# Constant loads, tile padding and start-up order in a three-layer fp32r kernel on one core

## The chip, the cores and the metric

The kernel runs on one core of a Trainium2 chip. The metric is the device time of one execution in microseconds (us). TensorE is called PE here, VectorE DVE, ScalarE ACT, GpSimd POOL, SyncE SP.

## The reference, cut to what matters

256 tokens of width 2048 go through three layers. Each layer is a norm, a large input projection, a mixer, and an output projection that is added to the residual; the last layer has also a gated feed-forward part.

```python
# first block: layer AB (banded and dilated attention), layer C (2-D neighbourhood attention)
x = x + (attention_ab(rmsnorm(x) @ w_in_ab) * silu(z)) @ w_out_ab
x = x + (attention_c(rmsnorm(x) @ w_in_c) * silu(z)) @ w_out_c
x = _rmsnorm(x, ln_f)
# second block
h = rmsnorm(x, norm1_w) @ w_in
x = x + concat(pool_mixer(h), gated_deltanet(h), rglru_mixer(h)) @ w_out
x = x + conv_ffn(rmsnorm(x, norm2_w), ffn_up, ffn_conv_w, ffn_down)
return rmsnorm(x, final_norm_w)
```

## The kernel before, in words

**Panels and chunks.** Every large product is cut into panels of 512 weight columns, 87 in all, numbered through the kernel: 0 to 12 `w_in_ab`, 13 to 16 `w_out_ab` (AT_OUT_AB is 13), 17 to 32 `w_in_c`, 33 to 36 `w_out_c` (AT_OUT_C is 33), 37 to 46 `w_in`, 47 to 50 `w_out`, and from 51 three groups of 12 for the feed-forward part. A panel has four chunks of 512 weight rows. I write (33,2) for chunk 2 of panel 33.

**Precision split.** Each fp32 weight chunk is split in two fp32r parts: ACT copies `raw` to `w_hi` (`split`, L335, the copy at L333), and DVE subtracts to get `w_lo` (L694 to L696). The activations are split the same way, into `act_hi`/`act_lo` or `ff_hi`/`ff_lo`. PE runs three of the four partial products, 48 matmuls for each chunk of an input projection (`panel`, L1308: the weight is stationary, 256 token columns move; L1321, L1323, L1329) and 24 for each chunk of an output projection (`deproject`, L1338: the activation is stationary, 512 weight columns move; L1356 to L1358). The panels 13 to 16 and 33 to 36 have `ff_hi`/`ff_lo` as the stationary operand, the other output panels `act_hi`/`act_lo`.

**Queues.** All order is written out by hand, with semaphores. SP loads the weights (`load`, L264): `raw` has one slot for each chunk of a panel, so the load of (g,c) waits for the DVE split of (g-1,c). ACT may write `w_hi` for (g,c) when PE has used chunk two before (`w_used`, L338), and DVE follows it. In an output panel PE starts a chunk only when both halves are there (L1350, L1351); in an input panel the `w_lo` matmuls come after those with `w_hi`.

**Start.** ACT issues three row tables (L636) and the sinks (L637), SP the identity (L291), `x` (L285) and the first weights (L289). PE waits for all five constants on one semaphore (L1659), transposes the tables, and ACT copies them to `params` (L639). Then each of the four chunks of panel 0 needs its quarter of `x` transposed by PE (`turn`, L1367), scaled into `act_hi` by ACT (`high_of_x`, L402) and into `act_lo` by DVE (`low_of_x`, L778). ACT also squares `x` (`squares_of`, L355) for the norm; DVE and ACT make the root (`variance`, `root`, `inverse_root`, `diagonal`), and PE spreads the scale over the partitions (`spread_scale`, L1395), after chunk 3 of panel 0.

**End of an attention layer.** `finish` (ACT L470, DVE L864) gates the heads with silu(z) and splits them into `ff_hi` and `ff_lo`, in four steps beside the last input panel and the first chunks of panel 13 or 33. Right behind it on ACT's queue stand loads: after the first layer `cmask` (L660) and the biases of two heads (`start_bias(1)`, eight small DMAs at L421), after the second `ln_f` (L670) and eight constants of the second block (`load_middle`, L488, issued at L500). Only then does `sum_into` (L388) go on with the weight split of (13,2) or (33,2).

**Tiles.** SBUF tiles are allocated one after the other (L113 to L134). In bytes for each partition all sizes are multiples of 64 but two: `params` (337 x 4 = 1348) and `gates` (172 x 4 = 688). Behind them lie `ones`, `scale_diag`, `token_scale`, `squared`, `proj`, `ff_gate`, `ff_hi` and `ff_lo`; ahead of them `resid`, `act_hi`, `act_lo`, `raw`, `w_hi`, `w_lo`, `work`, `ident`. The first tile starts at a multiple of 64 bytes, and the allocator rounds each start up to a multiple of 32. So all tiles behind `params` start 32 bytes past a multiple of 64, those ahead of it on one.

Of the kernel before, what the change touches and what calls it, by code (L numbers as in the profile page):

```python
# [24 lines left out]
P = 128  # L25
S = 256
D = 2048
NT = S // P
NK = D // P
PANEL = 512  # L30
QK = 4
HEADS = 16
A_HEADS = 8
# [68 lines left out]
def program(nc, a):  # L102

    ctx = ExitStack()
    with ctx:
        def sb(name, shape, dt=F32):
            return ctx.enter_context(nc.sbuf_tensor(name, shape, dt))
# [12 lines left out]
        ident = sb("ident", [P, P])  # L120
        params = sb("params", [P, PR_END])
        sinks = sb("sinks", [P, HEADS])
        small = sb("small", [P, 256])
        gates = sb("gates", [P, 172])
        ones = sb("ones", [P, P])
# [14 lines left out]
        x_landed = [sem(f"x_landed{i}") for i in range(4)]  # L140
        const_landed = sem("const_landed")
        raw_landed = [sem(f"raw_landed{c}") for c in range(4)]
# [4 lines left out]
        scale_diag_ready, scale_mm, scale_out = sem("scale_diag_ready"), sem("scale_mm"), sem("scale_out")  # L147
        turned, hi_act, lo_act = sem("turned"), sem("hi_act"), sem("lo_act")
        params_turned, params_ready = sem("params_turned"), sem("params_ready")
        z_ready = sem("z_ready")  # L150
# [112 lines left out]
        def _(sp):  # L263
# [19 lines left out]
            def load_x(i):  # L283
                cols = slice(i * PANEL, (i + 1) * PANEL)
                sp.dma_start(resid[:, :, cols], x_rows[:, :, cols]).then_inc(x_landed[i], 16)  # L285

            def load_first(c):
                src = a["w_in_ab"][c * 512:(c + 1) * 512, 0:PANEL].rearrange("(k p) n -> p k n", p=P)
                sp.dma_start(raw[:, c, :, :], src).then_inc(raw_landed[c], 16)  # L289

            sp.dma_start(ident[:], a["ident"]).then_inc(const_landed, 16)  # L291
            load_x(0)
            load_first(0)
            load_x(1)
            load_x(2)
            load_first(1)
            load_x(3)
            load_first(2)
            load_first(3)
            for p, (col, _) in enumerate(AB_PANELS):  # L300
                if p > 0:
                    load(False, p, rows_of(a["w_in_ab"]), slice(col, col + PANEL))
            panels(a["w_out_ab"], AT_OUT_AB, N_OUT)
            with sp.Fori(0, HEADS // 4) as j:
                for kind in range(3):
                    load(False, 3 * j + (AT_C + kind), rows_of(a["w_in_c"]), bass.ds(j * PANEL + kind * D, PANEL))
            panels(a["w_in_c"], AT_C + 12, 4, col0=3 * D)
            panels(a["w_out_c"], AT_OUT_C, N_OUT)
            for p, panel in enumerate(IN2_PANELS):
# [21 lines left out]
        def _(act):  # L331
# [55 lines left out]

            def sum_into(k, gp0, gain=None, x_hi=None, last=False):  # L388


                for i in range(N_OUT):
                    def between(c):
                        if c == 1 and i > 0:
                            summed_squares(k, gp0, i - 1)
                        if c == 2 and i > 0 and x_hi is not None:
                            high_of_x(k, i - 1, gain, x_hi)
                    panel(gp0 + i, between, last=last and i == N_OUT - 1)
                summed_squares(k, gp0, N_OUT - 1)
                if x_hi is not None:
                    high_of_x(k, N_OUT - 1, gain, x_hi)  # L400
# [22 lines left out]

            def start_bias(layer):
                if layer == 1:
                    act.wait_ge(rpb_spread, 16)
                for b in range(2):
                    load_bias(layer, b, b)

# [40 lines left out]
            def finish(layer, gp):  # L470
# [15 lines left out]
                high(layer, 3)  # L486

            def load_middle():  # L488

                for out, src in (  # L490
                        (work[:, 20:26, :], a["mid_consts"]),
                        (consts[:, M_POOLW:M_POOLW + POOL_G, :], a["pool_w_2"].rearrange("g c d -> c g d")),
                        (lru_w[:, 0:LRU_B, :], a["lru_wa_2"].rearrange("g c d -> c g d")),
                        (lru_w[:, LRU_B:2 * LRU_B, :], a["lru_wx_2"].rearrange("g c d -> c g d")),
                        (counts, a["counts"]),
                        (gate_w.rearrange("p (k n) -> p k n", k=NK),
                         a["w_in_2"][:, IN2_GATES:IN2_GATES + 12].rearrange("(k p) n -> p k n", p=P)),
                        (a_log, row_of(a["gdn_a_log_2"], GDN_H)),
                        (dt_bias, row_of(a["gdn_dt_bias_2"], GDN_H))):
                    act.dma_start(out, src).then_inc(mid_landed, 16)  # L500

# [132 lines left out]
            for i in range(3):  # L634
                rows = a[f"rows{i}"]
                act.dma_start(work[0:rows.shape[0], i, 0:P], rows).then_inc(const_landed, 16)  # L636
            act.dma_start(sinks[:, 0:A_HEADS], row_of(a["sink_a"], A_HEADS)).then_inc(const_landed, 16)  # L637
            act.wait_ge(params_turned, 3)
            copy(params[:, 0:PR_END], aux[:, 0, 0:PR_END]).then_inc(params_ready, 1)  # L639
            for c in range(4):  # L640
                high_of_x(0, c, PR_LN_AB, act_hi)
                split(0, c, first=c < 2)
                squares_of(0, c)
            root(0)
            for c in range(2):
                split(1, c)

            act.dma_start(rpb_rows, bass.AP(tensor=a["rpb_c"].tensor, offset=0,
                                            ap=[[RPB, HEADS], [0, GRID_W], [1, RPB]])).then_inc(rpb_spread, 16)
            start_bias(0)  # L650
            def first_root(k):
# [7 lines left out]
            finish(0, AT_AB + N_AB - 1)  # L659
            act.dma_start(cmask, a["cmask"]).then_inc(mask_landed, 16)  # L660
            start_bias(1)
            sum_into(1, AT_OUT_AB, PR_LN_C, act_hi)
            for p in range(3):
# [4 lines left out]
            finish(1, AT_C + N_C - 1)  # L668
            act.wait_ge(gated, 8)
            act.dma_start(lnf, row_of(a["ln_f"], D)).then_inc(lnf_landed, 16)  # L670
            load_middle()
            sum_into(2, AT_OUT_C, PR_N1, act_hi)
# [15 lines left out]
        def _(dve):  # L688
# [482 lines left out]

            chain.link(nc.vector.memset(ones[:], 1.0))
            chain.link(nc.vector.memset(sinks[:, A_HEADS:HEADS], NEG))
            dve.wait_ge(const_landed, 16 * 5)
            dve.wait_ge(params_ready, 1)
            for c in range(4):
                low_of_x(0, c, PR_LN_AB, act_hi, act_lo)
                split(0, c)
            variance(0, 1e-5)
            inverse_root(0)  # L1180
            diagonal(0, rstd)
            split(1, 0)
            scale_row(0)
            dve.wait_ge(w_used, 4)
            to_tile(AB_PANELS[0][1], 0)
            split(1, 1)
            for p in range(1, N_AB - 1):
# [117 lines left out]
        def _(pe):  # L1305
# [89 lines left out]
            def spread_scale(k):  # L1395
                pe.wait_ge(scale_diag_ready, k + 1)
                mm(aux[:, 1, 0:S], ones[:], scale_diag[:].rearrange("p t n -> p (t n)"), start=True, stop=True
                   ).then_inc(scale_mm, 1)

            def first_of(k, gp0=0):  # L1400

                def amid(c):
# [3 lines left out]
                    elif k > 0 and c == 0:  # L1406
                        turn_summed(k, gp0, 3)
                    if c == 3:
                        spread_scale(k)
# [248 lines left out]

            pe.wait_ge(const_landed, 16 * 5)  # L1659
            at = 0  # L1660
# [110 lines left out]
```

## Time and profile before

| | us |
|---|---|
| median of 3 runs (lowest, highest) | 2268.82 (2266.54, 2269.53) |
| the profiled execution's own time | 2265.74 |
| its span in the trace | 2263.5 |
| PE, PE weight loads, busy | 2189.7, 2070.8 |
| DVE, ACT, POOL, busy | 1261.8, 888.2, 206.6 |
| mean granted clock of TensorE | 0.989 of full speed |

The profile is one execution. Busy times are sums over the span; PE's matmuls overlap, so the spacing of their starts and the gaps between them tell more than the busy share.

### The profile page before, as it was taken

To read this page: it belongs to the slowest core of one execution; us is meant where nothing else is said; L and a number is where in the kernel's file an instruction comes from. 1 tells how busy PE (TensorE), PEld (TensorE's weight loads), DVE (VectorE), ACT (ScalarE), POOL (GpSimd) and SP (SyncE) were. 2 spreads that over 40 slices of the span, in tenths; PEclk is the share of its full clock that TensorE was granted. 3 is DMA by queue.
4 is the path that set the end of the run, shared out by engine and by line. 5 is a ranking of instruction groups with operands and counts; after the bars stand their busy time and mean duration, and the time that the engine had idled before them with its cause. 6 is when DMAs were issued, how large, how long until landed. Compare 5 with 4: busy or idle time off the path is not lost.

```text
span 2263.5 us, 36570 instructions
## 1 busy us (share of the span) xinstructions
PE 2189.7 (97%) x15751; PEld 2070.8 (91%) x15751; DVE 1261.8 (56%) x1265; ACT 888.2 (39%) x850; POOL 206.6 (9%) x242
## 2 busy tenths in 40 slices
PE   6999999999999998999999889999999999999997
PEld 6999998899999997789999878999989999899986
DVE  4555555544555555565588645565445655466554
ACT  4344334443333344453546324434333333333333
POOL 0101100002022110002000420001100011000200
PEclk9999999999999999999999999999999999999999
DMA  6755544555555546554554105555555555555553
GB/s 221 220 176 171 168 163 163 186 173 182 167 168 168 181 156 201 173 181 149 168 168 150 56 9 188 194 186 187 186 188 185 185 187 186 191 182 186 186 187 111
DMA packets 212140, 386.66 MB, mean 171 GB/s; under 512 B 26058, under 2 KB 29595, under 8 KB 211739
## 3 DMA queue, kind: packets, MB, share of 16 engines
q1 hardware_dynamic: 185552, 369.19, 49.6%
q10 hardware_dynamic: 26443, 15.30, 2.4%
q8 instruction: 120, 1.97, 0.4%
q14 instruction: 25, 0.20, 0.0%
HBM read 382.36 MB, written 4.00 MB: 171 GB/s over the span
## 4 chain that ended last, share of the span: by engine, by line
PE 90%; DVE 4%; ACT 3%; ACTq 1%; issue 1%; POOL 0%; DMA 0%; DVEq 0%; POOLq 0%
PE acc L1321 20%; PE acc L1323 20%; PE acc L1329 20%; PE acc L1356 8%; PE acc L1357 8%; PE acc L1358 7%; ACT w_hi L333 2%; DVE w_lo L696 1%; PE aux L1448 1%; ACTq L421 1%; PE aux L1426 1%; PE aux L1610 1%; PE aux L1619 1%; PE aux L1373 1%; PE aux L1437 1%
## 5 line engine op out<-in xcount | busy, mean ns | idle before, releaser
L696 DVE TENSOR_TENSOR w_lo<-raw,w_hi 128x2048 fp32r<-128x2048 f32 x348 | 810.9, 2331 | 795.9 <-ACT w_hi L333 795.2
L333 ACT ACTIVATE w_hi<-raw 128x2048 fp32r<-128x2048 f32 x348 | 666.1, 1915 | 1079.2 <-PE acc L1329 752.5
L1321 PE MATMUL acc<-act_hi,w_hi 128*128 128x256 f32 x2496 | 618.4, 288 | 8.5 <-ACT w_hi L333 8.5
L1323 PE MATMUL acc<-act_lo,w_hi 128*128 128x256 f32 x2496 | 608.9, 284 | 0.0
L1321 PEld LDWEIGHTS acc<-act_hi,w_hi 128*128 128x128 f32 x2496 | 481.5, 193 | 10.7 <-DVE act_lo L783 9.4
L1323 PEld LDWEIGHTS acc<-act_lo,w_hi 128*128 128x128 f32 x2496 | 481.7, 193 | 1.2
L1321 PE MATMUL acc<-ff_hi,w_hi 128*128 128x256 f32 x1536 | 372.9, 283 | 0.6 <-issue 0.6
L1323 PE MATMUL acc<-ff_lo,w_hi 128*128 128x256 f32 x1536 | 372.6, 281 | 0.0
L1329 PE MATMUL acc<-act_hi,w_lo 128*128 128x256 f32 x2496 | 325.8, 283 | 0.0
L1329 PEld LDWEIGHTS acc<-act_hi,w_lo 128*128 128x128 f32 x2496 | 310.8, 192 | 0.2
L1323 PEld LDWEIGHTS acc<-ff_lo,w_hi 128*128 128x128 f32 x1536 | 289.6, 189 | 0.1
L1321 PEld LDWEIGHTS acc<-ff_hi,w_hi 128*128 128x128 f32 x1536 | 288.7, 188 | 1.1 <-issue 1.0
L1329 PE MATMUL acc<-ff_hi,w_lo 128*128 128x256 f32 x1536 | 199.9, 282 | 0.0
L1356 PE MATMUL acc<-w_hi,act_hi 128*128 128x512 f32 x512 | 199.9, 390 | 0.0
L1358 PE MATMUL acc<-w_hi,act_lo 128*128 128x512 f32 x512 | 199.3, 389 | 0.0
L1357 PE MATMUL acc<-w_lo,act_hi 128*128 128x512 f32 x512 | 199.2, 389 | 0.0
L1329 PEld LDWEIGHTS acc<-ff_hi,w_lo 128*128 128x128 f32 x1536 | 191.1, 188 | 0.1
L1231 POOL COPY work<-proj 128x256 f32<-128x256 f32 (+1 forms) x96 | 63.8, 704 | 669.8 <-DVE proj L718 569.0
L1356 PE MATMUL acc<-w_hi,ff_hi 128*128 128x512 f32 x256 | 103.9, 406 | 18.7 <-DVE w_lo L696 18.7
L1356 PEld LDWEIGHTS acc<-w_hi,act_hi 128*128 128x128 f32 x512 | 96.1, 188 | 20.1 <-issue 0.2
L1358 PEld LDWEIGHTS acc<-w_hi,act_lo 128*128 128x128 f32 x512 | 96.1, 188 | 20.0
L1357 PEld LDWEIGHTS acc<-w_lo,act_hi 128*128 128x128 f32 x512 | 96.1, 188 | 19.9 <-issue 0.2
(247 smaller groups left out, 1680.7 us busy)
## 6 DMA issues: line engine op xcount, KB each, us to landing
raw<-in_ffn_up SPq DMA_DIRECT2D x96, 1024.0 KB, 5.2
raw<-in_w_in_c SPq DMA_DIRECT2D x64, 1024.0 KB, 5.6
raw<-in_w_in_ab SPq DMA_DIRECT2D x52, 1024.0 KB, 5.1
raw<-in_ffn_down SPq DMA_DIRECT2D x48, 1024.0 KB, 5.1
raw<-in_w_in SPq DMA_DIRECT2D x40, 1024.0 KB, 5.1
raw<-in_w_out_ab SPq DMA_DIRECT2D x16, 1024.0 KB, 5.1
raw<-in_w_out_c SPq DMA_DIRECT2D x16, 1024.0 KB, 5.0
raw<-in_w_out SPq DMA_DIRECT2D x16, 1024.0 KB, 5.1
```

The lines of the kernel that those rows point to most:

```text
L333: copy = lambda out, in_, **k: nc.scalar.activation(out, in_, ACT.Copy, **k)
L421: act.dma_start(bias(b)[r * GRID_W:(r + 1) * GRID_W, t, :] .rearrange("p (a k) -> p a k", a=4), src).then_inc(rpb_landed[b], 16)
L696: tt(w_lo[:, c % 2], raw[:, c], w_hi[:, c % 2].bitcast(F32), ALU.subtract).then_inc(lo_ready, 1)
L1231: ins = copy(out, proj[:, tile, :])
L1321: mm(out(j), w, hi[:, 4 * c + k, :], start=(c == 0 and k == 0 and j % 2 == 0), stop=False, skip_group_check=True)
L1323: mm(out(j), w, lo[:, 4 * c + k, :], start=False, stop=False, skip_group_check=True)
L1329: ins = mm(out(j), w_lo[:, c % 2, k, j * P:(j + 1) * P], hi[:, 4 * c + k, :], start=False, stop=(c == 3 and k == QK - 1), skip_group_check ...
L1356: mm(out(t), x_hi, w_hi[:, c % 2, k, :], start=(c == 0 and k == 0), stop=False)
L1357: mm(out(t), x_hi, w_lo[:, c % 2, k, :], start=False, stop=False)
L1358: ins = mm(out(t), x_lo, w_hi[:, c % 2, k, :], start=False, stop=(c == 3 and k == QK - 1))
L1373: ins = nc.tensor.transpose(aux[:, 2 * (i % 2) + j // 2, (j % 2) * S + t * P:(j % 2) * S + (t + 1) * P], rows[:, t, (4 * i + j) * P:(4 * i ...
L1426: ins = mm(aux[:, b, t * S:(t + 1) * S], qs(b)[:, t * P:(t + 1) * P], ks(b), start=(t == 0), stop=True, skip_group_check=True)
```

## The change

Six edits. (1) `params` and `gates` are padded to 352 and 176 columns. (2) The sinks have a semaphore of their own, and the wait for constants is for four DMAs. (3) SP's first loads alternate `x` and weights. (4) ACT squares `x` in pairs, the splits of panel 1 come ahead of the root, and `spread_scale(0)` moves behind chunk 0 of panel 1. (5) `cmask` is issued by SP at panel 2; the biases of the first two heads are issued by ACT at the last chunk of panels 14 and 15; `ln_f` and the constants of the second block are issued by SP, behind the loads of panel 33 and a wait for the last gating. (6) PE runs 16 matmuls on `ones` ahead of its first wait for data.

```diff
-        params = sb("params", [P, PR_END])
+        params = sb("params", [P, -(-PR_END // 16) * 16])
-        gates = sb("gates", [P, 172])
+        gates = sb("gates", [P, 176])
...
@@ SP
+            def load_middle():
...
+                    sp.dma_start(out, src).then_inc(mid_landed, 16)
...
-            load_x(0)
-            load_first(0)
-            load_x(1)
-            load_x(2)
-            load_first(1)
-            load_x(3)
-            load_first(2)
-            load_first(3)
+            for c in range(4):
+                load_x(c)
+                load_first(c)
             for p, (col, _) in enumerate(AB_PANELS):
                 if p > 0:
                     load(False, p, rows_of(a["w_in_ab"]), slice(col, col + PANEL))
+                if p == 2:
+                    sp.dma_start(cmask, a["cmask"]).then_inc(mask_landed, 16)
...
-            panels(a["w_out_c"], AT_OUT_C, N_OUT)
+            load(False, AT_OUT_C, rows_of(a["w_out_c"]), slice(0, PANEL))
+            sp.wait_ge(gated, 8)
+            sp.dma_start(lnf, row_of(a["ln_f"], D)).then_inc(lnf_landed, 16)
+            load_middle()
+            for i in range(1, N_OUT):
+                load(False, AT_OUT_C + i, rows_of(a["w_out_c"]), slice(i * PANEL, (i + 1) * PANEL))
@@ ACT
+                        if also:
+                            also(i, c)
...
-            def start_bias(layer):
-                if layer == 1:
-                    act.wait_ge(rpb_spread, 16)
-                for b in range(2):
-                    load_bias(layer, b, b)
+            def first_biases(i, c):
+
+                if c == 3 and 1 <= i <= 2:
+                    load_bias(1, i - 1, i - 1)
...
-            act.dma_start(sinks[:, 0:A_HEADS], row_of(a["sink_a"], A_HEADS)).then_inc(const_landed, 16)
+            act.dma_start(sinks[:, 0:A_HEADS], row_of(a["sink_a"], A_HEADS)).then_inc(sinks_landed, 16)
...
                 split(0, c, first=c < 2)
-                squares_of(0, c)
+                if c % 2 == 1:
+                    squares_of(0, c - 1)
+                    squares_of(0, c)
+            split(1, 0)
             root(0)
-            for c in range(2):
-                split(1, c)
+            split(1, 1)
...
-            act.dma_start(cmask, a["cmask"]).then_inc(mask_landed, 16)
-            start_bias(1)
-            sum_into(1, AT_OUT_AB, PR_LN_C, act_hi)
+            act.wait_ge(rpb_spread, 16)
+            sum_into(1, AT_OUT_AB, PR_LN_C, act_hi, first_biases)
...
-            act.wait_ge(gated, 8)
-            act.dma_start(lnf, row_of(a["ln_f"], D)).then_inc(lnf_landed, 16)
-            load_middle()
             sum_into(2, AT_OUT_C, PR_N1, act_hi)
@@ DVE
             variance(0, 1e-5)
+            split(1, 0)
             inverse_root(0)
             diagonal(0, rstd)
-            split(1, 0)
+            split(1, 1)
             scale_row(0)
             dve.wait_ge(w_used, 4)
             to_tile(AB_PANELS[0][1], 0)
-            split(1, 1)
+            dve.wait_ge(sinks_landed, 16)
@@ PE
+            def warm_up():
+
+                pe.wait_ge(ones_ready, 1)
+                for i in range(16):
+                    mm(aux[:, 3, 0:P], ones[:], ones[:], start=True, stop=True)
...
-                    if c == 3:
+                    if k > 0 and c == 3:
                         spread_scale(k)
...
-                    for p in range(1, 4):
+                    panel(1, 1, *x, amid=lambda c: spread_scale(0) if c == 0 else None)
+                    for p in range(2, 4):
                         panel(p, p % 2, *x, heads(p))
...
-            pe.wait_ge(const_landed, 16 * 5)
+            warm_up()
+            pe.wait_ge(const_landed, 16 * 4)
```

## Rows read from the trace of the kernel before

**Rows 1.** The page: busy us (share of the span) xinstructions
```profile
PE 2189.7 (97%) x15751; PEld 2070.8 (91%) x15751; DVE 1261.8 (56%) x1265; ACT 888.2 (39%) x850; POOL 206.6 (9%) x242
```

**Rows 2.** PE's waits: line waited for, us in total, times, longest
```profile
PE acc L1356 <- DVE w_lo L696: 18.7, 2, 13.1
PE aux L1663 <- DMA sinks<-in_sink_a: 9.1, 1, 9.1
```

**Rows 3.** ACT, and one row of DVE: start us, us, line, operation, idle before
```profile
372.01 1.06 ACT L333 ACTIVATE ff_hi<-proj 128x1024 fp32r<-128x1024 f32 x1 [2.73 <-DVE proj L857]
372.39 5.35 ACTq L421 DMA_DIRECT2D work<-scratch_rpb_rows  x8
373.10 1.23 DVE L861 TENSOR_TENSOR ff_lo<-proj,ff_hi 128x1024 fp32r<-128x1024 f32 x1 [1.12 <-ACT ff_hi L333]
377.84 3.71 ACT L333 ACTIVATE w_hi<-raw 128x2048 fp32r<-128x2048 f32 x2 [4.78 <-issue]
...
890.03 1.06 ACT L333 ACTIVATE ff_hi<-proj 128x1024 fp32r<-128x1024 f32 x1 [2.73 <-DVE proj L857]
890.04 0.34 ACTq L670 DMA_DIRECT2D proj<-in_ln_f  x1
...
891.96 3.42 ACTq L500 DMA_DIRECT2D work<-in_lru_wx  x1
...
902.74 0.46 ACTq L500 DMA_DIRECT2D small<-in_gdn_dt_bias  x1
903.30 3.71 ACT L333 ACTIVATE w_hi<-raw 128x2048 fp32r<-128x2048 f32 x2 [12.20 <-issue]
```

**Rows 4.** Stretches: PE busy (x), PEld, DVE, ACT, POOL, granted clock, DMA share, GB/s
```profile
365.20:376.61 11.41, 11.41 (x50) 8.86 (x48) 7.41 (x6) 4.87 (x4) 0.00 (x0) 1.00 0.65 221
...
382.22:388.28 6.06, 6.06 (x14) 4.82 (x15) 2.06 (x1) 0.00 (x0) 0.00 (x0) 0.50 0.83 282
388.28:407.00 18.72, 18.72 (x81) 15.05 (x80) 8.10 (x4) 5.76 (x3) 0.00 (x0) 1.00 0.38 134
894.63:907.68 13.05, 0.00 (x1) 0.03 (x1) 2.44 (x2) 3.71 (x2) 0.00 (x0) 0.59 0.70 194
907.68:910.53 2.85, 2.85 (x7) 2.27 (x8) 2.05 (x1) 0.00 (x0) 0.00 (x0) 0.50 0.52 162
2166.00:2230.00 64.00, 64.00 (x284) 53.03 (x283) 32.96 (x17) 24.13 (x21) 4.95 (x2) 1.00 0.56 190
55.05:72.33 17.28, 17.28 (x146) 17.28 (x145) 6.88 (x3) 5.75 (x3) 0.00 (x0) 1.00 1.05 309
1459.13:1510.97 51.84, 51.84 (x435) 51.84 (x434) 34.13 (x41) 17.25 (x9) 0.00 (x0) 1.00 0.57 182
```

**Rows 5.** The page: split groups, xcount | busy, mean ns; output matmuls on ff_hi
```profile
L696 DVE TENSOR_TENSOR w_lo<-raw,w_hi 128x2048 fp32r<-128x2048 f32 x348 | 810.9, 2331 | 795.9 <-ACT w_hi L333 795.2
L333 ACT ACTIVATE w_hi<-raw 128x2048 fp32r<-128x2048 f32 x348 | 666.1, 1915 | 1079.2 <-PE acc L1329 752.5
L1356 PE MATMUL acc<-w_hi,ff_hi 128*128 128x512 f32 x256 | 103.9, 406 | 18.7 <-DVE w_lo L696 18.7
```

**Rows 6.** SP in time at panel 34; the page: w_out_c loads, us to landing
```profile
881.28 6.99 SPq L271 DMA_DIRECT2D raw<-in_w_out_c  x2
...
raw<-in_w_out_c SPq DMA_DIRECT2D x16, 1024.0 KB, 5.0
```

**Rows 7.** The chain at the start, in order: start us, us, what
```profile
2.22 6.81 DMA sinks<-in_sink_a
...
10.44 1.98 PE aux L1373 x8
12.45 1.57 ACT act_hi L333 x4
14.02 1.81 ACT w_hi L333
```

**Rows 8.** ACT in panel 0: start us, us, line, operation, idle before
```profile
22.56 1.57 ACT L333 ACTIVATE act_hi<-aux,params 128x256 fp32r<-128x256 f32 x4 [5.53 <-PE aux L1373]
...
44.15 1.28 ACT L380 ACT_TABLE_LOAD   x1
```

More of the change, by code:

```diff
@@ L140, in program @@
         x_landed = [sem(f"x_landed{i}") for i in range(4)]
-        const_landed = sem("const_landed")
+        const_landed, sinks_landed = sem("const_landed"), sem("sinks_landed")
         raw_landed = [sem(f"raw_landed{c}") for c in range(4)]
@@ L148, in program @@
         turned, hi_act, lo_act = sem("turned"), sem("hi_act"), sem("lo_act")
+        ones_ready = sem("ones_ready")
         params_turned, params_ready = sem("params_turned"), sem("params_ready")
@@ L285, in load_x @@
                 sp.dma_start(resid[:, :, cols], x_rows[:, :, cols]).then_inc(x_landed[i], 16)
+            def load_middle():
+                for out, src in (
+                        (work[:, 20:26, :], a["mid_consts"]),
+                        (consts[:, M_POOLW:M_POOLW + POOL_G, :], a["pool_w_2"].rearrange("g c d -> c g d")),
+                        (lru_w[:, 0:LRU_B, :], a["lru_wa_2"].rearrange("g c d -> c g d")),
+                        (lru_w[:, LRU_B:2 * LRU_B, :], a["lru_wx_2"].rearrange("g c d -> c g d")),
+                        (counts, a["counts"]),
+                        (gate_w.rearrange("p (k n) -> p k n", k=NK),
+                         a["w_in_2"][:, IN2_GATES:IN2_GATES + 12].rearrange("(k p) n -> p k n", p=P)),
+                        (a_log, row_of(a["gdn_a_log_2"], GDN_H)),
+                        (dt_bias, row_of(a["gdn_dt_bias_2"], GDN_H))):
+                    sp.dma_start(out, src).then_inc(mid_landed, 16)
             def load_first(c):
@@ L386, in summed_squares, with sum_into @@
                     squares_f(i)
-            def sum_into(k, gp0, gain=None, x_hi=None, last=False):
+            def sum_into(k, gp0, gain=None, x_hi=None, also=None, last=False):
                 for i in range(N_OUT):
@@ L486, in finish @@
                 high(layer, 3)
[L488 to L500, printed above, removed]
             def mixers(p, c):
@@ L642, in _ @@
                 split(0, c, first=c < 2)
-                squares_of(0, c)
+                if c % 2 == 1:
+                    squares_of(0, c - 1)
+                    squares_of(0, c)
+            split(1, 0)
             root(0)
-            for c in range(2):
-                split(1, c)
+            split(1, 1)
             act.dma_start(rpb_rows, bass.AP(tensor=a["rpb_c"].tensor, offset=0,
                                             ap=[[RPB, HEADS], [0, GRID_W], [1, RPB]])).then_inc(rpb_spread, 16)
-            start_bias(0)
+            for b in range(2):
+                load_bias(0, b, b)
             def first_root(k):
@@ L1170, in ffn @@
                 chain.n = base + 8 * FFN_GROUPS
-            chain.link(nc.vector.memset(ones[:], 1.0))
+            nc.vector.memset(ones[:], 1.0).then_inc(ones_ready, 1)
             chain.link(nc.vector.memset(sinks[:, A_HEADS:HEADS], NEG))
-            dve.wait_ge(const_landed, 16 * 5)
+            dve.wait_ge(const_landed, 16 * 4)
             dve.wait_ge(params_ready, 1)
```

## The prediction

> **What bounds the kernel now.** I read the busy times first. PE works 2189.7 us, 97% of the span, and no other engine reaches 60% [rows 1]. So a change gains only where it closes a gap of PE or makes its matmuls closer spaced. The view of PE's waits comes next: two waits of output panels for `w_lo` make 18.7 us, the longest 13.1, and the first wait for constants is 9.1 us [rows 2]. These are the places that the change touches. ACT in time shows who is late in the two. At 373.07 ACT is through with `ff_hi`, but it then issues DMAs until 377.74, and only then splits (13,2). At 891.09 it is through again, but it issues nine DMAs from 890.04 to 903.20 and splits (33,2) at 903.30 [rows 3]. "issue" as the releaser says that ACT waited for nothing but its own queue. Last I read stretches of PE. Its gaps are 376.61 to 382.22 (5.6 us) and 894.63 to 907.68 (13.05 us). Behind each the granted clock is half (1.2 GHz): for 6.06 us with 14 matmuls, and for 2.85 us with 7 [rows 4].
>
> **Biases and `cmask` off the path (stall A, panel 13).** Without the issues ACT splits (13,2) at 373.1, done at 375.0 (1.92 us). DVE has `ff_lo` until 374.3 and follows with 2.33 us, to 377.35 [rows 3, 5]. PE starts the chunk at about 377.45 instead of 382.22: 4.8 us gained. It would have been ready at 376.1, so a gap of 1.4 us stays, too short in my reading to lose the clock. The 14 slow matmuls took 6.06 us; at 0.234 each they take 3.3, so 2.8 more comes back [rows 4]. Together 7.6. The biases are now issued behind the splits (14,1) and (15,1). Eight took 5.35 us, so four take 2.7 [rows 3]. ACT's next split is due one chunk (24 matmuls, 5.45 us) after the last one began; 1.92 + 2.7 = 4.6 fits, with 0.8 to spare. If the cover were gone, each of the two places would cost up to 2.7. `cmask` at panel 2 is one more issue on SP, in front of a load with four chunks of slack: nothing.
>
> **`ln_f` and the constants on SP (stall B, panels 33 and 34).** (33,2) is now split by ACT at 891.1 to 893.0 and by DVE, behind `ff_lo`, until 895.35. PE starts it at 895.45, not 907.68: 12.2 us gained; the 7 slow matmuls give back 2.85 - 7 x 0.234 = 1.2 [rows 3, 4]. But now SP stands still until the last gating, 890.0, and then issues nine DMAs before the load of (34,0), which went out at 881.28 before [rows 3, 6]. What holds those issues is not ACT but the transfers: single ones took 3.42 us against 0.46 [rows 3]. On ACT they took 13.2 us. SP starts with an empty queue, since no weight load runs beside them, and I take 12.1: the load of (34,0) is issued at 902.1 and lands 5.0 to 5.3 later, 907.3 [rows 6]. Then ACT needs 1.92 and DVE 2.33 [rows 5], and PE starts (34,0) at 911.6. It was ready at 895.45 + 2 x 5.45 = 906.35: a new gap of 5.3 us. The gap of 5.6 in stall A cost 2.8 in clock; I take 2.0 here [rows 4]. Net gain of B: 12.2 + 1.2 - 5.3 - 2.0 = 6.1. Bounds: were each issue 0.46 us, SP would be through at 894.2, but the load would still queue behind the transfers, which the blocked issues show to last until about 902, and with some 2.5 us of its own land no earlier than about 904.5 (an estimate), a gap of 2.5 and no clock loss (gain 10.9); at the other end a landing at 910 makes a gap of 8 and 2.8 of clock (gain 2.6). (34,1) to (34,3) are issued right behind and land two or three us apart, ahead of their splits, which are 5.45 apart. Stalled with (34,0) are DVE's addition for panel 33 and the gain by `ln_f`, together 2.45 us on DVE behind that split; they end before (34,1) needs DVE.
>
> **Padding.** 1348 and 688 bytes become 1408 and 704, so `ff_hi` and `ff_lo` move from 32 bytes past a multiple of 64 onto one. Output matmuls with `ff_hi` as stationary take 18.72 us for 80 weight loads, 234.0 ns each; those with `act_hi`, which lies ahead of the odd sizes, 64.00 / 283 = 226.1 [rows 4]. ACT and DVE have the same to do in both, so the address is what is left. There are 3 x 256 such matmuls [rows 5]. The first 48 of both panels 13 and 33 end in a wait anyway; 672 x 7.9 ns = 5.3 us gained, between 0 (the address is not the cause) and 6.1. As the moving operand the offset costs nothing: three chunks on `act_hi` take 17.28 us and nine on `ff_hi` 51.84, both 5.76 a chunk [rows 4]. So the feed-forward panels stay. I take nothing for DVE, ACT and POOL, which have no share in the bound there.
>
> The Trainium skill (SBUF — State Buffer, Specifications) says that SBUF has lines of 16 bytes. By it a tile 32 bytes off would lose nothing and this term would be zero, which is rival (a); the trace, with 234.0 against 226.1, does not agree so far.
>
> **The start.** PE's first work waits for the sinks, landed at 9.03 [rows 7]. The last table is issued one slot (0.5 us) ahead of them, so PE starts at about 8.5: 0.5 gained, between 0 and 1. The warm-up runs from about 1.1. A cold transpose took 1.98 / 8 = 0.25 us [rows 7], so 16 matmuls end near 5. Then PE idles for 3.5 us until the tables land, and in this trace the clock was down after idle stretches of 5.6 and 13 us [rows 4]. I take 0; if it held, the 8 transposes and the first 17 matmuls would run at twice the rate, worth 2.5. It can't cost, as it ends 3.5 us before PE has work. Squares in pairs: ACT sat idle 5.53 us ahead of `act_hi` of chunk 1 [rows 8], which two more squares don't fill: nothing. At chunk 3 the pair ends 1.25 later, the split (1,0) starts at 45.4 rather than 45.65, and the root with its table load (1.28, [rows 8]) comes behind it, while `spread_scale` is now needed only at 53: nothing. The order of SP's loads: `x` for chunks 2 and 3 lands later but more than ten us before its use: nothing.
>
> **The sum.** 7.6 + 6.1 + 5.3 + 0.5 = 19.5 us off the profiled execution's 2265.74, which makes 2246.2. That execution is 3.1 faster than the median of the runs; for a median I take the gain off 2268.82: 2249.3.
>
> **Rivals.** (a) The offset from a multiple of 64 is not the cause, so that the padding doesn't do what it says: A, B and the start alone, 14.2 us, 2254.6. The 226.1 of one operand and 234.0 of the other speak against it; that the trace has each at one address only, far from each other, speaks for it. Chance 0.13. (b) The load of (34,0) is late by so much that B gains nothing: the landing would be near 913, if SP's nine issues took longer than ACT's or the first load ran slowly behind 48-byte pieces. 19.5 - 6.1 = 13.4: 2255.4. For it speaks that the wait takes the place of the one removed, against it that DMA was free of weight loads then. Chance 0.12. (c) The new gap is small, 2.5 us and no lower clock: 19.5 + 4.8 = 24.3, 2244.5. Chance 0.13. (d) The warm-up holds the clock: 2.5 more, 2246.8. Chance 0.05. (e) Slower: the same place, SP's queue ahead of (34,0). Each us of delay past 907.3 is a us of PE. To end above 2273.4 it must eat 19.5 and 4.6 more, so land 24 us later, at 931, with SP issuing for 36 us. On ACT the nine issues took 13.2 us [rows 3], so that is far off. Chance 0.02. My forecast keeps 0.55.
>
> **Range and chances.** From (c) with a good part of (d), 2242, to (b) with some run-to-run spread, 2258. A measurement of this kernel can tell about 0.2%, 4.5 us, from no change. All cases but (e) end beyond that; a loss of A and B in part together could end within it. Faster 0.95, same 0.03, slower 0.02.
>
> **What would show it.** Right: PE waits at (13,2) and (33,2) of 1 to 2 us each; a new wait of 4 to 7 us at the first L1356 of panel 34, released by the split and, behind it, by a landing; spacing of 226 to 227 ns in panels 14 to 16; input chunks still 5.76; PE's first instruction on data at 8.5 and the clock low at panel 0 as before. Wrong: no wait at panel 34, a wait in panels 14 or 15 behind ACT's DMA issues, a spacing that stays at 234, or input chunks that change.

## The result and the profile after the change

The changed kernel takes 2252.14 us, the median of four runs (2250.54 to 2253.89), beside 2268.56 for the kernel before: a ratio of 0.9929, 95% interval 0.9916 to 0.9941. Predicted were 2249.3, range 2242 to 2258. The profiled execution took 2250.63 us with a span of 2248.4; against 2265.74 that is 15.1 us less. The total fits; three of its four terms have to be looked at one by one.

The page of after: busy times and a line of the DMA queues. PE's busy time is the same as before [rows 1], since the warm-up added 6.5 us of work to it (`no_warm_up`, below, has 2184.0 us).

```profile
PE 2189.7 (97%) x15783; PEld 2072.0 (92%) x15783; DVE 1261.3 (56%) x1265; ACT 888.7 (40%) x850; POOL 206.7 (9%) x242
...
q8 instruction: 122, 2.00, 0.4%
```

PE's waits of after (line waited for: us in total, times, longest). Output panels wait for `w_lo` three times with 6.8 us in all, not twice with 18.7 [rows 2]. The wait for the sinks has gone. A group has grown in which PE waits for nothing that the profile shows: it was one wait of 0.6 us before, and is 4.5 us now, the longest 3.9.

```profile
PE acc L1325 <- ACT w_hi L350: 8.5, 4, 3.5
PE aux L1447 <- DVE work L834: 7.4, 6, 3.0
PE acc L1360 <- DVE w_lo L699: 6.8, 3, 5.2
PE acc L1325 <- issue: 4.5, 2, 3.9
```

Stall A in time, ACT and then DVE of after. They answer to [rows 3]: ACT goes straight from `ff_hi` to the split of (13,2).

```profile
369.68 1.06 ACT L350 ACTIVATE ff_hi<-proj 128x1024 fp32r<-128x1024 f32 x1 [2.73 <-DVE proj L860]
370.64 1.90 ACT L350 ACTIVATE w_hi<-raw 128x2048 fp32r<-128x2048 f32 x1
...
370.77 1.23 DVE L864 TENSOR_TENSOR ff_lo<-proj,ff_hi 128x1024 fp32r<-128x1024 f32 x1 [1.13 <-ACT ff_hi L350]
372.58 2.29 DVE L699 TENSOR_TENSOR w_lo<-raw,w_hi 128x2048 fp32r<-128x2048 f32 x1 [0.58 <-ACT w_hi L350]
```

Stall B in time, SP, ACT and DVE of after. SP's nine issues begin at 879.76, and the loads of panel 34 go out from 891.75; the split of (34,0) waits for a landing, DVE for the split, and PE starts the chunk at 901.71.

```profile
879.76 0.34 SPq L322 DMA_DIRECT2D proj<-in_ln_f  x1
...
883.61 2.97 SPq L300 DMA_DIRECT2D work<-in_counts  x1
...
887.10 4.13 SPq L300 DMA_DIRECT2D small<-in_gdn_a_log  x1
...
891.75 10.21 SPq L272 DMA_DIRECT2D raw<-in_w_out_c  x5
...
897.33 1.91 ACT L350 ACTIVATE w_hi<-raw 128x2048 fp32r<-128x2048 f32 x1 [11.05 <-DMA raw<-in_w_out_c]
...
899.27 2.29 DVE L699 TENSOR_TENSOR w_lo<-raw,w_hi 128x2048 fp32r<-128x2048 f32 x1 [10.66 <-ACT w_hi L350]
```

Stretches of after, with the columns of [rows 4]: the new gap at panel 13 and what follows it, the gap at panel 34 and what follows, 94 spacings of output matmuls on `ff_hi`/`ff_lo`, 1005 of input matmuls on them in the first feed-forward group and all 1535 in the second, and the new stop of PE with what follows it.

```profile
373.79:375.02 1.23, 0.40 (x3) 0.03 (x1) 1.08 (x1) 0.74 (x1) 0.00 (x0) 1.00 0.00 0
375.02:381.00 5.98, 5.98 (x26) 4.84 (x27) 2.29 (x1) 1.23 (x2) 0.00 (x0) 1.00 0.69 218
...
896.15:901.71 5.56, 0.40 (x2) 0.03 (x1) 2.44 (x2) 3.59 (x2) 0.00 (x0) 0.93 1.05 396
901.71:907.80 6.09, 6.09 (x14) 4.76 (x15) 4.41 (x3) 0.23 (x1) 0.00 (x0) 0.50 1.03 367
...
421.77:443.70 21.93, 21.93 (x96) 17.64 (x94) 11.87 (x9) 9.50 (x12) 0.00 (x0) 1.00 0.60 198
1440.77:1559.91 119.14, 119.14 (x1006) 119.14 (x1005) 74.68 (x79) 43.55 (x24) 6.92 (x4) 1.00 0.57 185
1689.12:1873.32 184.20, 184.20 (x1537) 184.19 (x1535) 105.75 (x92) 65.20 (x36) 15.86 (x6) 1.00 0.57 183
...
1962.45:1966.68 4.23, 0.29 (x4) 0.19 (x2) 2.29 (x1) 0.25 (x1) 0.00 (x0) 0.91 0.54 181
1966.68:1969.30 2.62, 2.62 (x13) 2.62 (x13) 0.00 (x0) 0.00 (x0) 0.00 (x0) 0.50 0.96 341
```

The gap at panel 13 is 1.23 us from start to start, and the clock stays up. The output matmuls are spaced 21.93 / 94 = 233.3 ns, where I had expected 226 to 227. The input matmuls are spaced 119.14 / 1005 = 118.5, and I had expected no change from 120.0. That holds for the first feed-forward group (panels 51 to 58) and the third (75 to 82). In the second (63 to 70) they stay at 184.20 / 1535 = 120.0, in this kernel and in all others with this padding and nothing moved behind it, `pad_only` too, though the tiles lie at the same addresses in all three groups. The stop at 1962.45 has no counterpart before. PE in time shows the start:

```profile
1.06 6.49 PE L1408 MATMUL aux<-ones 128*128 128x128 f32 x32 [1.06 <-DVE ones L1175]
8.30 0.51 PE L1675 MATMUL aux<-ident,work 121*128 121x121 f32 x3 [0.74 <-DMA work<-in_rows]
9.35 1.09 PE L1377 MATMUL aux<-ident,resid 128*128 128x128 f32 x8 [0.54 <-ACT params L350]
13.99 0.55 PE L1325 MATMUL acc<-act_hi,w_hi 128*128 128x256 f32 x1 [3.55 <-ACT w_hi L350]
```

The warm-up ends at 7.55, not at 5; its 16 matmuls are 32 records. The eight transposes of `x` then take 1.09 us, not 1.98 [rows 7], and the first weight matmul starts at 13.99, not 15.96.

**Where the time went.** I follow DVE's start of the same `w_lo` split in both traces; the lead is how much sooner it is after. It is 2.3 us at panel 2 and at 13, 10.4 at panel 17 (so 8.0 in panels 13 to 16), 10.3 at 32, 16.2 at 37 (6.0 around stall B), 16.4 at 51, 18.4 at 63 and still at 75, then 13.3 at 76 (5.1 lost by the stop), and 15.1 in the last panel.

### The profile page after: what moved, and what is told of

Same layout as the page of the kernel before. It is cut to its first block, busy times and chain, and to the rows that moved or that the text cites. A ratio compares the mean times of both kernels' runs of the same rounds, so it can differ in the third digit from the quotient of the medians.

```text
span 2248.4 us, 36582 instructions
## 1 busy us (share of the span) xinstructions
PE 2189.7 (97%) x15783; PEld 2072.0 (92%) x15783; DVE 1261.3 (56%) x1265; ACT 888.7 (40%) x850; POOL 206.7 (9%) x242
## 4 chain that ended last, share of the span: by engine, by line
PE 90%; DVE 4%; ACT 3%; issue 1%; ACTq 1%; POOL 1%; DMA 1%; SPq 1%; DVEq 0%; POOLq 0%
PE acc L1325 20%; PE acc L1327 20%; PE acc L1333 20%; PE acc L1360 7%; PE acc L1361 7%; PE acc L1362 7%; ACT w_hi L350 2%; DVE w_lo L699 1%; PE aux L1458 1%; PE aux L1436 1%; PE aux L1621 1%; PE aux L1630 1%; PE aux L1377 1%; PE aux L1447 1%; PE acc L1629 1%
```

## The experiments

**The padding alone.** `pad_only` is the kernel before with the padding and nothing else, to size that term and see where it acts.

```diff
-        params = sb("params", [P, PR_END])
+        params = sb("params", [P, -(-PR_END // 16) * 16])
-        gates = sb("gates", [P, 172])
+        gates = sb("gates", [P, 176])
```

> The kernel before with edit 1 (the padding) alone. Theory P (the distance from a multiple of 64 bytes sets the spacing, as predicted): output matmuls on ff_hi at 226 to 227 ns, 5 to 6 us faster than before. Theory R (what counts is where the two operands lie to each other, at a coarser grain than 64 bytes; the padding only moves that by chance): spacing 232 to 233 ns as in the changed kernel, 1.2 us from there, input panels on ff_hi at 119.4 instead of 120.0 ns, 2.7 us from there, 3 to 4 us in all.

It took 2265.84 us (2261.64 to 2268.26, 11 runs) beside 2269.16: ratio 0.999, interval 0.9981 to 0.9999. So the padding gives 3.3 us, with an interval of about 0.2 to 4.3. The leads of its trace tell why a median of whole runs is a blunt measure here: it gains 1.3 to 2.0 us at each of four places that the padding touches, and loses 2.9 between the first splits of panels 47 and 48, beside the mixers, where the clock was low for 20.5 us and in the trace of before for 13.7. Its stretches show the small change of spacing of after, without any other edit:

```profile
407.69:429.53 21.84, 21.84 (x96) 17.71 (x94) 11.87 (x9) 9.78 (x12) 0.00 (x0) 1.00 0.53 188
...
1456.83:1559.96 103.13, 103.13 (x872) 103.13 (x870) 66.52 (x74) 37.80 (x21) 5.27 (x2) 1.00 0.57 184
```

232.3 and 118.5 ns (the latter in the first and third feed-forward group only), beside 234.0 and 120.0 before [rows 4]. So a multiple of 64 isn't what makes an output matmul take 226.

**What does set the spacing.** `micro_offsets` leaves out the reference's computation and runs only matmuls of the two forms, out of tiles whose distance is chosen. Groups of 48 (output form) and 64 (input form) run without a break.

```diff
+x = sb("x", [P, 17 * 512], FR); w = sb("w", [P, 17 * 512], FR)
...
+for o in OFFSETS:            # bytes that the activation is moved; 0: same place modulo 2048
+    output_form(o // 4)      # activation stationary, 512 weight columns move
+for m in (8, 16, 32, 64):    # columns that the weight is moved instead
+    output_form(0, m)
+for o in OFFSETS:
+    input_form(o // 4)       # weight stationary, 256 activation columns move
```

> Not the reference's computation: only matmuls in the form of an output panel (16 groups of 48, stationary operand moved by 0, 4, 16, 32, 48, 64, 96, 128, 192, 256, 384, 512, 768, 1024, 1280, 1536 bytes past a multiple of 2048; 4 groups with the moving operand at 32, 64, 128, 256 bytes) and of an input panel (16 groups of 64, moving operand moved by the same), with no other engine at work. Theory P: 226 to 227 ns at every multiple of 64, about 234 at the others. Theory R: spacing depends on the offset beyond 64 bytes too, 226 to 227 at 0 only, 231 to 234 at others, and in input form 119 to 120 ns everywhere. If other engines' work made the difference in the kernels, the spacing is the same at all offsets.

Mean ns from start to start, with the activation that many bytes further (the output form at 0 is left out: it is the first group of the trace, and its first matmuls stand 427 ns apart; 512, 768, 1024, 1280 and 1536 are alike, and in the input form 0 too; each value is one group in one execution):

```
offset          4    16    32    48    64    96   128   192   256   384   512
output form  232.4 233.3 233.2 233.3 233.3 234.4 232.6 228.9 226.8 232.2 226.7
input form   123.1 116.7 116.8 118.4 117.8 119.8 118.7 113.7 119.8 118.7 120.0
weight moved: 32 bytes 233.4, 64: 228.9, 128: 232.2, 256: 227.4 (output form)
```

Two of the groups in the trace, with the columns of [rows 4]: 48 output matmuls at 64, and 64 input matmuls at 192.

```profile
76.01:87.20 11.19, 11.19 (x49) 9.02 (x48) 0.00 (x0) 0.00 (x0) 0.00 (x0) 1.00 0.00 0
...
302.20:309.49 7.29, 7.29 (x67) 7.29 (x65) 0.00 (x0) 0.00 (x0) 0.00 (x0) 1.00 0.01 2
```

Here the time depends on the distance of the two operands modulo 256 bytes: 384 gives what 128 gives, and 256 and 512 what a multiple of 2048 gives. Moving the weight by 64 gives what moving the activation by 192 gives (both 228.9), so it is the distance and not an address. At 64 from the same place, where both addresses are multiples of 64, an output matmul takes 233.3, one of the worst values. It fits the kernel: `ff_hi` was 96 from the weights (234.4 and 119.8 here; 234.0 and 120.0 in before) and is 128 after the change (232.6 and 118.7 here; 233.3 and 118.5 in after). It doesn't fit the second feed-forward group of after, where the same distance of 128 gives 120.0, so in the kernel something besides the distance has a part. My expectation that the input form would stand at 119 to 120 everywhere was wrong too. The Trainium skill's lines of 16 bytes (SBUF — State Buffer, Specifications) would leave every multiple of 16 alike; the runs don't agree.

`micro_fine` is the same kernel with other offsets, around 192.

> Not the reference's computation: micro_offsets again with a finer grid, the moved operand at 0 and at 136 to 248 bytes in steps of 8, and at 188 and 196. If 192 is the one good place: input form 113 to 114 at 192 alone and 117 and more beside it. If it is the middle of a band: 113 to 115 from about 176 to 208. Output form: 229 at 192, 231 to 234 elsewhere.

Input form: 176 gives 119.2, 188 gives 120.0, 192 gives 113.6, 196 gives 120.0, 208 gives 119.1. Output form: 228.4 at 240, 228.9 at 192, 230 at 176, 230.7 at 200, so in that form 192 isn't the only good place, which I had not expected. So 192 is one sharp good place for input matmuls, not the bottom of a wide valley.

**Two uses of it in the kernel.** `same_phase` puts `ff_hi`/`ff_lo` at the weights' place modulo 256, and `phase_192` puts both pairs 192 past it.

```diff
# same_phase
+        sb("gap_ff", [P, 32])       # 128 bytes, ahead of proj
# phase_192
+        sb("gap_w", [P, 16])        # 64 bytes, between act_lo and raw
+        sb("gap_ff", [P, 16])       # 64 bytes, ahead of proj
```

> The kernel after with one 128-byte tile more ahead of proj, so that ff_hi and ff_lo have the same address as the weights modulo 256. The theory that the distance modulo 256 sets the spacing expects the output matmuls on ff_hi at 226.8 ns (232.6 after) and the input matmuls on ff_hi at 120.0 (119.3 after): 720 x 5.8 ns = 4.2 us less and 24 panels x 192 x 0.7 ns = 3.2 us more, in all 1 us less, 2251. The theory that any multiple of 64 is as good as another expects no change of either spacing.

`same_phase` took 2255.57 (2251.83 to 2256.31, 5 runs) beside 2266.61: ratio 0.9945, interval 0.9931 to 0.9959. Its output and input stretches:

```profile
398.38:419.70 21.32, 21.32 (x95) 17.64 (x94) 11.87 (x9) 9.50 (x12) 0.00 (x0) 1.00 0.62 206
...
1438.87:1559.94 121.07, 121.07 (x1012) 121.07 (x1010) 75.30 (x79) 43.55 (x24) 7.57 (x4) 1.00 0.57 183
```

21.32 / 94 = 226.8 and 121.07 / 1010 = 119.9, both as expected. It doesn't pay: beside after the output matmuls win 672 x 6 = 4.0 us, and the input matmuls lose about as much, 3072 x 1.3 = 4.0, in the two feed-forward groups in which after has 118.7 (the second has 120.0 in both). It was expected 1 us faster than after and is 3.4 slower by the medians; the two intervals overlap, so that isn't a clear difference.

> The changed kernel with two tiles of 64 bytes put in, ahead of raw and ahead of proj, so that act_hi, act_lo, ff_hi and ff_lo all lie 192 bytes past w_hi and w_lo, counted in steps of 256. Theory R in the form that micro_offsets gave (the distance of the two operands modulo 256 bytes sets the spacing): 12096 input matmuls at 113.7 instead of 119.2 to 120, 2304 output matmuls at 228.9 instead of 226.7 (act) and 232.6 (ff). That is 7488 x 6.3 + 4608 x 5.6 + 768 x 3.7 - 1536 x 2.2 = 72 us less, 2180, if PE stays the bound. If the kernel's other traffic or the splits on DVE set the pace instead, the spacing falls less, or PE waits for w_lo: over 2200. Theory P: nothing, or 1 to 2 us slower.

`phase_192` took 2220.50 (2217.33 to 2230.55, 5 runs) beside 2269.03: ratio 0.9794, interval 0.9773 to 0.9814. That is 31.6 us faster than after by the medians (24.3 by the two profiled executions; its runs spread over 13 us), and well short of the 2180 expected. The stretches say why:

```profile
390.96:412.49 21.53, 21.53 (x96) 17.65 (x94) 11.87 (x9) 9.50 (x12) 0.00 (x0) 1.00 0.61 199
1401.04:1417.34 16.30, 16.30 (x147) 16.30 (x144) 8.34 (x12) 7.42 (x8) 0.00 (x0) 1.00 0.75 257
1418.00:1559.92 141.92, 141.92 (x1207) 141.92 (x1206) 87.70 (x85) 52.13 (x29) 13.23 (x6) 1.00 0.56 186
```

Output matmuls take 229.0. Input matmuls take 113.2 in the first stretch and 117.7 in the next; over the trace they sit at 113 or at 118 and change only where something interrupts PE's row of matmuls. What picks one of the two wasn't found. The output form has two levels as well: in this trace the last four panels run at 233.3 ns, at the same distance at which `combined`, below, has 228.9 there.

**The start and the stop of PE.** `no_warm_up` is the kernel after without the 16 matmuls, to see what they give.

```diff
-            warm_up()
             pe.wait_ge(const_landed, 16 * 4)
```

> The changed kernel without edit 6 (the 16 warm-up matmuls). If the warm-up alone gave the faster clock at the start: PE's first transposes take 1.98 us again instead of 1.10, the first weight matmul comes 1.0 to 1.2 us later, at 15.1. If the stop of PE of 4.2 us at 1962 in the changed kernel comes from where its instructions lie in memory (the warm-up moves them by 32 matmul records), it vanishes here: 4 to 5 us faster than the changed kernel in all, some 2247.5. If that stop is a chance event of single executions, this kernel is 1 us slower than the changed one, 2253.

2248.29 (2247.48 to 2250.97, 4 runs) beside 2269.16: ratio 0.9913, interval 0.9897 to 0.9928, so 3.9 us faster without it than with it by the medians, 2.0 by the profiled executions. The intervals of the two ratios overlap, so the traces have to carry this: a lead 1.7 smaller at panel 2, and no 5.1 us lost at panel 75. PE in time at the start, and the page's line of the DMA queue for instructions:

```profile
8.05 0.82 PE L1674 MATMUL aux<-ident,work 121*128 121x121 f32 x3 [8.05 <-DMA work<-in_rows]
9.42 1.97 PE L1377 MATMUL aux<-ident,resid 128*128 128x128 f32 x8 [0.54 <-ACT params L350]
14.94 0.55 PE L1325 MATMUL acc<-act_hi,w_hi 128*128 128x256 f32 x1 [3.55 <-ACT w_hi L350]
...
q8 instruction: 120, 1.97, 0.4%
```

The transposes are slow again and the lead over before is 0.6 us at panel 2, 1.7 less than with the warm-up. But the stop in the third feed-forward group is gone: PE's longest wait in an input panel for nothing but its own queue is 0.6 us, not 3.9. In after it sits ten matmuls into panel 75, right behind the jump back of a loop. Three more kernels ask whether the stop comes from the work of the warm-up or from the length of PE's program.

```diff
# warm_8
-                for i in range(16):
+                for i in range(8):
# short_16; short_32 has range(32) besides
-                    mm(aux[:, 3, 0:P], ones[:], ones[:], start=True, stop=True)
+                    mm(aux[:, 3, 0:16], ones[:], ones[:, 0:16], start=True, stop=True)
```

> The changed kernel with 8 warm-up matmuls instead of 16. If the stop of PE in the third feed-forward group comes from where the instructions lie, moving them by 16 records changes or removes it: up to 5.6 us faster by that. The warm-up then ends near 4.3, four us before the tables land, and the clock should be low for the transposes, as without it: 1 to 1.7 us slower by that. Together 2247 to 2250; if the stop stays as it is, 2253 to 2254.

> The kernel after with as many warm-up matmuls, each over 16 columns instead of 128, so that PE's program keeps its length and does less work at the start. If the stop of about 4 us in the third feed-forward group comes from the length of PE's program (where its loops lie), it stays, and the time is 2252 to 2254. If it comes from the work of the warm-up (the clock, the time at which PE runs), it goes, and the time is about 2248. At the start I expect a shorter warm-up and the gap ahead of the transposes that goes with it.

> The kernel after with 32 warm-up matmuls over 16 columns, so that PE's program is longer by 16 matmuls with their weight loads. If the stop comes from where the loops lie it changes: larger, smaller (2.08 us with 8 fewer, none with 16 fewer), or at another place; if only the presence of a warm-up matters, it stays at 4 us.

`warm_8` took 2252.61 (5 runs; ratio 0.9931, interval 0.9917 to 0.9944), `short_16` 2254.57 (4 runs; 0.9939, 0.9923 to 0.9956), `short_32` 2257.18 (4 runs; 0.995, 0.9934 to 0.9967). The wait for PE's own queue in each, in this order:

```profile
PE acc L1325 <- issue: 2.5, 2, 1.8
```

```profile
PE acc L1325 <- issue: 4.3, 2, 3.5
```

```profile
PE acc L1325 <- issue: 0.5, 1, 0.5
```

`short_16` does less work per matmul and has the length of after: the stop stays (3.83 us from start to start, at 1966.96). `short_32` has a warm-up too, and a longer one, but the stop is gone (no gap over 1 us behind 1337 us). `warm_8` has a stop of 2.08 us. So it isn't the warm-up's work that makes PE stop 1.95 ms later, but how far its instructions push those behind them: 16 matmuls 4.2 us, 8 matmuls 2.1, none or 32 nothing. A stop of 3.8 to 4.2 us stands at this place in the traces of all six kernels here with 16 such matmuls.

The DMA queue for instructions tells what PE waits for. It carries 122 packets of 16 KB (2.00 MB) in after, `short_16` and `warm_8`, 121 in `short_32` and 120 without a warm-up. In after one of them lies inside the stop: it runs from 1964.29 to 1965.24, and PE, idle since 1962.7, starts again at 1966.68. The queue's line for 1964.25 to 1965.30:

```profile
q8 instruction: 1, 0.02, 5.6%
```

In three more traces the end of such a packet and PE's restart belong together in the same way: 1969.37 and 1970.77 in `warm_8`, 1969.56 and 1970.79 in `short_16`, 1957.76 and 1959.19 in `later_constants`, below. So PE restarts 1.2 to 1.4 us behind a packet of code in all four, and the likely cause is that it waits for this code; why the packet comes late in one layout and in time in another stays open. The Trainium skill (Runtime: NRT & Kernel Launch, Instruction fetch mechanics) says that a taken branch whose target isn't in the part of the code at hand has to wait for its fetch; the place of the stop, ten matmuls behind a jump, and the packet inside it agree with that.

The same runs tell of the start. `warm_8` and `short_16`, PE in time:

```profile
1.06 3.79 PE L1408 MATMUL aux<-ones 128*128 128x128 f32 x16 [1.06 <-DVE ones L1175]
8.41 0.82 PE L1675 MATMUL aux<-ident,work 121*128 121x121 f32 x3 [3.56 <-DMA work<-in_rows]
9.77 1.97 PE L1377 MATMUL aux<-ident,resid 128*128 128x128 f32 x8 [0.55 <-ACT params L350]
```

```profile
1.06 7.01 PE L1408 MATMUL aux<-ones 128*128 128x16 f32 x32 [1.06 <-DVE ones L1175]
...
9.46 1.97 PE L1377 MATMUL aux<-ident,resid 128*128 128x128 f32 x8 [0.54 <-ACT params L350]
```

In neither do the transposes become fast. The records of a warm-up stand 0.213 us apart, over 16 columns as over 128; in after the last six speed up, to 0.112, and those of `short_16` and `short_32` never do. So `short_32` kept PE busy until 14.9 and its transposes came 6.6 us late, which with the stop gone makes it the slowest of these. What the warm-up is worth isn't constant either: the lead at panel 2 is 2.3 in after, but 2.0, 1.7 and 1.1 in `same_phase`, `biases_back` and `later_constants`, which start alike.

**The two stalls.** `biases_back` is after with the eight bias issues ahead of the split (13,2) again; `cmask` stays on SP.

```diff
-            sum_into(1, AT_OUT_AB, PR_LN_C, act_hi, first_biases)
+            for b in range(2):
+                load_bias(1, b, b)
+            sum_into(1, AT_OUT_AB, PR_LN_C, act_hi)
```

> The changed kernel with the eight bias DMAs of the first two heads issued by ACT ahead of the weight split of (13,2) again, but cmask still on SP. If stall A was ACT's issue time, PE waits there 1.2 + 5.4 us less what lay in ACT's idle time, about 5.2 more than in the changed kernel, and the clock falls behind it (another 2.8): 7 to 8 us slower, 2260. If the clock alone made it, 3 us slower.

2262.43 (2257.43 to 2264.94, 5 runs) beside 2269.03: ratio 0.9965, interval 0.9952 to 0.9979, 10.3 us slower than after. ACT in time:

```profile
370.28 1.06 ACT L350 ACTIVATE ff_hi<-proj 128x1024 fp32r<-128x1024 f32 x1 [2.74 <-DVE proj L862]
370.28 5.35 ACTq L440 DMA_DIRECT2D work<-scratch_rpb_rows  x8
375.74 3.71 ACT L350 ACTIVATE w_hi<-raw 128x2048 fp32r<-128x2048 f32 x2 [4.40 <-PE acc L1364]
```

The stall is back, 5.73 us from start to start, and the lower clock behind it. By the leads panels 13 to 16 give 1.7 us in this kernel and 8.0 in after: this edit alone is worth 6.3 of the 7.6 forecast for A. Most of the rest of the 10.3 lies in panels 43 to 48, which the edit doesn't touch: there it falls 4.5 us behind after, and the clock is low for 27.3 us in all, beside 17.1 in after. `no_warm_up` loses 2.9 there in the same way, with 23.9. So a few us between two of these kernels can come from how long the clock stays low around the waits of the mixers.

`later_constants` is after with SP's loads of panel 34 ahead of the wait for the gating and the nine constant loads.

```diff
-            load(False, AT_OUT_C, rows_of(a["w_out_c"]), slice(0, PANEL))
+            for i in range(2):
+                load(False, AT_OUT_C + i, rows_of(a["w_out_c"]), slice(i * PANEL, (i + 1) * PANEL))
             sp.wait_ge(gated, 8)
...
-            for i in range(1, N_OUT):
+            for i in range(2, N_OUT):
```

> The changed kernel with SP's loads of panel 34 ahead of the wait for the gating and of the nine constant loads. If the new wait at (34,0) comes only from the place in SP's queue: no wait of PE there (5.2 us less), no lower clock behind it (2.8 us less), 7 to 8 us faster than the changed kernel, 2244 to 2245. If the transfers of the constants slow the loads or the gain by ln_f comes late on DVE instead, a wait of PE at panel 35 takes its place and less than half of that is won.

2244.03 (2241.86 to 2245.23, 4 runs) beside 2269.16: ratio 0.9891, interval 0.9876 to 0.9906, 8.1 us faster than after, and by the leads 8.1 between panels 33 and 37. The wait at (34,0) has gone. The load of (34,3) has to wait for its slot ahead of them, so the constants are issued from 889.91 on, and nothing waits for them. SP in time:

```profile
878.36 11.51 SPq L272 DMA_DIRECT2D raw<-in_w_out_c  x3
889.91 0.50 SPq L323 DMA_DIRECT2D proj<-in_ln_f  x1
```

**All that helped.** `combined` is `phase_192` with the order of `later_constants` and without the warm-up (its edits are those shown above).

> The kernel after with three things at once: act_hi/act_lo and ff_hi/ff_lo 192 bytes past the weights modulo 256, SP's loads of panel 34 ahead of the constants, and no warm-up matmuls. If the three gains are independent: 2252.1 minus 31.7 (the distance), 8.1 (the order) and 3.9 (no warm-up) = 2208.5. If the stop of PE in the third feed-forward group belongs to the place of the loop's code and not to the warm-up, it stays (it stood in the two single runs that kept the warm-up and not in the one that left it out) and the time is about 2212 to 2214.

2214.63 (2208.07 to 2216.82, 5 runs) beside 2266.61: ratio 0.9757, interval 0.9739 to 0.9776. It is the fastest kernel here, 2.4% below the one before, and PE has no stop in the third group. Beside `phase_192` it gains 5.9 us by the medians, where 12.0 were expected, and 11.7 by the spans of the two profiled executions (2224.1 and 2212.4). The runs of both spread over 9 to 13 us, more than those of after, so whether the three gains simply add isn't settled. Its waits of PE begin with a group that had 7.4 us in after (and 11.4 in `phase_192`): in the attention panels a faster PE waits longer for DVE.

```profile
PE aux L1450 <- DVE work L837: 12.0, 7, 3.3
```

## Why the prediction was right and wrong

**Stall A: right.** 7.6 us were forecast. The lead grew by 8.0 in panels 13 to 16, of which the padding accounts for some tenths. The gap that stayed was 1.23 us from start to start (1.4 forecast), with no lower clock, and no wait came in panels 14 and 15 behind the moved biases.

**Stall B: right in sum, its clock term too small.** Net 6.1 was forecast and 6.0 came. Each step held: SP's nine issues took 11.9 us (12.1), the chunk landed 5 to 5.6 us behind its issue, and the new gap was 5.56 from start to start, 5.3 as a gap. But the clock was low behind it from 901.0 to 907.8, and PE's 14 matmuls from 901.71 on took 6.1 us instead of 3.3, which costs 2.8; I had said 2.0. The part that hides this is the padding, some tenths in panels 33 to 36. `later_constants`, 8.1 us faster, is the price of both: 5.3 + 2.8 = 8.1. Rival (c), a small gap, was wrong.

**The padding: near in sum, by luck; wrong in cause and place.** The failed step is "so the address is what is left". I had compared `act_hi` (226.1) and `ff_hi` (234.0) and read the difference as a property of one address. It belongs to the distance of two operands, the activation's and the weight's, modulo 256. `act_hi` is fast because it lies at the weights' own place. The change moved `ff_hi` from 96 to 128, which gives 1.7 ns, so 672 x 1.7 = 1.1 us instead of 5.3. The second step that failed is "so the feed-forward panels stay": both forms had 5.76 us a chunk, 120.0 ns, but 120.0 is what distances 0 and 96 give alike; 128 gives 118.5 to 118.7. The lead grows by 2.0 us in the first feed-forward group and by 1.8 in the third, and not at all in the second, which stays at 120.0; why, no run shows. Together some 4.9 by the leads, and 3.3 in `pad_only`. Two of the prediction's own signs of being wrong had come: a spacing that stays near 234, and input chunks that change. Rival (a) had the cause right (not the multiple of 64) and the term wrong, as it set it to zero.

**The start: mis-sized.** 0.5 was forecast and 2.3 came. Without the warm-up the lead is 0.6, so the term for the tables, and nothing for the order of SP's loads and the squares in pairs, was right in sum; the three weren't tried apart. The failed step is "16 matmuls end near 5": each is two records, 0.20 us on the mean, so they end at 7.55 and leave PE idle for 0.74 us, not 3.5. The transposes then run at 0.14 us each, not 0.25. Rival (d) had this, with 2.5 for it; 1.7 came, since the clock is at half again from 13.5 to 16.9, behind a wait of 3.55 us.

**"It can't cost": wrong.** I priced the warm-up only where it stands. It costs 2 to 4 us on balance (`no_warm_up`; 3.4 by these two terms): 1.7 gained at the start, and 5.1 lost in panel 75, by a stop of 4.2 us and 13 matmuls at half the clock behind it. This was in none of my rivals. It is also why the total fell 2.9 us short of the forecast: with 5.1 taken out, the kernel would be at some 2247 (an estimate). That the total lies in the range thus owes something to luck: the start brought 1.8 us more than forecast, and the stop took 5.1.

## What to carry to other kernels

Price an idle time together with what the clock does behind it, and look one step further for the wait that takes its place: both stalls here came out that way to within a microsecond. When two tiles differ in speed, compare what the instruction reads together, not one tile's address, and measure it alone over a row of distances before it is called alignment; the row showed a place worth ten times the padding. Instructions added at the start can move a loop further on, so look over the whole trace for new waits on nothing.

## What was not expected of the hardware

- Measured alone, the spacing of fp32r matmuls depends on the distance of stationary and moving operand modulo 256 bytes: for 512 columns 226.7 ns at 0, 228.9 at 192 and 228.4 to 234.4 elsewhere; for 256 columns 120.0 at 0 and 113.7 at 192, with 188 and 196 back at 120.0.
- In the kernel one distance can have two levels: 113 or 118 ns at 192, kept until PE is interrupted; 118.7 or 120.0 at 128, by the feed-forward group; 228.9 or 233.3 for the output form at 192.
- PE can stop for 4.2 us behind a loop's jump, depending on how many instructions stand ahead of the loop: 4.2, 2.1 or nothing with 16, 8 and 0 or 32 fp32 matmuls. It starts again 1.2 to 1.4 us behind a 16 KB packet of the instruction queue.
- The granted clock of a stretch ahead of a trace's first clock record is shown as 1.00, even where matmuls run at half speed. That record stands at 19.6 us in before and at 6.7 in after. In before, the first matmuls on weights stand 0.21 us apart from 15.96 to 19.7, and the record shows this:

```profile
15.90:19.00 3.10, 3.04 (x14) 3.07 (x15) 2.24 (x1) 1.13 (x4) 0.00 (x0) 1.00 1.06 389
```
